# RWKV-7 inverse in 32x32 blocks, with the block transposes on VectorE

## The reference

```
S = S * w_t + (S a_t) b_t^T + v_t k_t^T        a_t = -kk_t, b_t = kk_t * iclr_t
y_t = S r_t                                    (latent tokens only)
w_t = exp(-exp(-softplus(-(w0 + tanh(wd) @ w2)) - 0.5)),  iclr_t = sigmoid(a0 + ad @ a2)
```

## Time and profile before

| | us |
|---|---|
| median of 3 runs | 1727.96 |
| lowest and highest | 1724.86, 1730.27 |
| span of the profiled execution | 1725.2 |
| TensorE busy (matmul) in that span | 1595.0 |
| VectorE, ScalarE, GpSimd busy | 706.5, 565.5, 871.3 |

### The profile page before, as it was taken

One profiled execution on the slowest core, in us unless ns is written; L12 is line 12 of the kernel. 1 busy time (PEld: TensorE's weight loads), 2 busy tenths in 40 slices (PEclk: granted clock), 3 DMA queues, 4 the chain that ended last, 5 costly groups with the idle time before them and its releaser, 6 DMA issues. The chain is left out here.

```text
span 1725.2 us, 35315 instructions
## 1 busy us (share of the span) xinstructions
PE 1595.0 (92%) x15534; PEld 1293.4 (75%) x15534; DVE 706.5 (41%) x1049; ACT 565.5 (33%) x810; POOL 871.3 (51%) x407
## 2 busy tenths in 40 slices
PE   4899999988989888989999999989989899999996
PEld 2688868767677786748888888858867588888885
DVE  1433246668676755462121212640374521212134
ACT  3423256543534322243232323132222432323230
POOL 1532213198776833248888888734433344444441
PEclk9999899999999999999999999889989999999998
DMA  7322001032222222224444443222221122222221
GB/s 319 125 77 78 1 1 50 2 116 86 101 77 77 79 75 81 74 74 147 146 147 146 146 146 146 73 74 98 92 78 50 64 102 94 93 93 96 96 94 49
DMA packets 23617, 162.15 MB, mean 94 GB/s; under 512 B 2624, under 2 KB 3264, under 8 KB 4800
## 3 DMA queue, kind: packets, MB, share of 16 engines
q1 hardware_dynamic: 21904, 154.09, 24.8%
q10 hardware_dynamic: 1584, 6.13, 0.9%
HBM read 157.71 MB, written 2.10 MB: 93 GB/s over the span
## 5 line engine op out<-in xcount | busy, mean ns | idle before, releaser
L221 POOL TENSOR_TENSOR v<-raw,v 128x1024 fp32r<-128x1024 f32 x160 | 389.7, 2459 | 421.6 <-ACT v L209 397.4
L238 PE MATMUL bank<-hm,v 128*128 128x512 f32 x2112 | 488.9, 393 | 15.0 <-DVE hm L1985 12.8
L238 PEld LDWEIGHTS bank<-hm,v 128*128 128x128 f32 x2112 | 400.0, 190 | 104.1 <-issue 17.8
L238 PE MATMUL bank<-hid,v 128*128 128x512 f32 x1536 | 349.5, 389 | 0.0
L238 PEld LDWEIGHTS bank<-hid,v 128*128 128x128 f32 x1536 | 288.3, 188 | 59.8
L209 ACT ACTIVATE v<-raw 128x2048 fp32r<-128x2048 f32 x77 | 147.6, 1917 | 420.8 <-PE bank L238 420.7
L2116 DVE TENSOR_TENSOR bank<-bank,rl 128x512 f32<-128x512 f32 x64 | 44.8, 700 | 275.1 <-ACT rl L2095 275.1
L1047 POOL TENSOR_TENSOR raw<-raw,cs 128x2048 f32<-128x2048 f32 x24 | 86.8, 3615 | 104.3 <-issue 64.3
L221 POOL TENSOR_TENSOR w<-raw,w 128x1024 fp32r<-128x1024 f32 x22 | 54.2, 2485 | 136.4 <-ACT w L209 136.4
L540 PE MATMUL bank<-h,w 128*128 128x512 f32 x600 | 109.6, 344 | 0.0
L540 PEld LDWEIGHTS bank<-h,w 128*128 128x128 f32 x600 | 93.9, 191 | 15.1 <-issue 1.1
(11 more groups left out here) (319 smaller groups left out, 2273.6 us busy)
## 6 DMA issues: line engine op xcount, KB each, us to landing
raw<-w_in SPq DMA_DIRECT2D x119, 1024.0 KB, 4.8
mraw<-wm_in SPq DMA_DIRECT2D x16, 1024.0 KB, 4.7
raw<-wm_in SPq DMA_DIRECT2D x3, 1024.0 KB, 16.2
xres<-x_in ACTq DMA_DIRECT2D x1, 2048.0 KB, 8.7
yb<-wm_in SPq DMA_DIRECT2D x2, 1024.0 KB, 19.6
mixed_in<-wm_in SPq DMA_DIRECT2D x2, 1024.0 KB, 23.5
xres<-x_in SPq DMA_DIRECT2D x1, 2048.0 KB, 8.9
out_T<-xres ACTq DMA_DIRECT2D x8, 256.0 KB, 2.0
```

The source lines that it names most:

```text
L221: i = nc.gpsimd.tensor_tensor(W[1][n % 2][:, k:k + 4], raw[n % 2][:, k:k + 4], W[0][n % 2][:, k:k + 4].bitcast(F32), SUB)
L238: last = nc.tensor.matmul(bank(b(s, m), 0, hi - lo), W[w][s][:, k, m * P:(m + 1) * P], H[h][:, k, lo:hi], start=(k == 0 and w == h == 0), ...
```

## The change

The inverse is taken in 32x32 blocks. Levels 0 to 3 (LVL = 4) invert only the diagonal 32x32 blocks: X, its transpose XTB and the level's product W1 have 384 elements a partition and direction instead of 768; products use 32 rows and 32 columns of TensorE each, 48 a group instead of 24, and all four row and column positions write one PSUM bank. The transpose of X is VectorE's 32x32 block transpose from SBUF to SBUF (`blocks_turned`); TensorE's transposes and ScalarE's `inverse_rows` go. The last level becomes two products: `corner_product` (the off-diagonal block of L times X) and `lower_columns` (the lower 32 columns of XT, with an identity that ScalarE puts beside the corner), each 24 products a direction; the left columns are a ScalarE copy with the upper half as scale.

In `chunk_matrices` item `L` computes diagonal 32x32 blocks alone (48 products instead of 24), and `LT` lies by head in the two banks. The low-rank products run two a level in levels 0 to 3, through banks 4, 5 and 7. ScalarE runs gates 0 to 4, the exponentials of direction 0, gates 5 and 6, the exponentials of direction 1, gate 7, the keys, then the left columns. The bonus product moves behind the corner products. The constant table is 191 columns narrower.

```diff
-    LVL = 5
+    LVL = 4
+    B = 32
...
+    def lora_at(i):
+        lo, hi = SEG[PIECES[i][1]]
+        return bank((4, 5, 7)[i % 3], 0, hi - lo)
...
-                if i:
-                    pe.wait_ge(sig_ready, NP * p + i)
-                nc.tensor.matmul(bank(7, 0, hi - lo), lw[r, p, kind, :], lora[r, kind, lo:hi], start=True, stop=True)\
-                    .then_inc(lora_done, 1)
+                if j:
+                    pe.wait_ge(sig_ready, NP * p + 2 * j - 1)
+                for d in range(2):
+                    r = slice(d * HD, (d + 1) * HD)
+                    nc.tensor.matmul(lora_at(2 * j + d), lw[r, p, kind, :], lora[r, kind, lo:hi], start=True, stop=True)\
+                        .then_inc(lora_done, 1)
...
+            def diagonal_blocks(i, d):
+                for g in range(GD):
+                    for c in range(2):
+                        for b in range(2):
+                            for h in range(2):
+                                at, cx = g * B, c ^ d
+                                t, ta = (2 * g + c) * Q + b * B, (2 * g + cx) * Q + b * B
+                                last = nc.tensor.matmul(ring(i, h, at, at + B)[quarter_of(cx, b)],
+                                                        AT_[half(h), d, ta:ta + B], BT[half(h), d, t:t + B],
+                                                        start=True, stop=True)
...
             def first_product(p, lv, d):
-                for g in range(GD):
+                for m in range(MS):
                     for q in range(2):
-                        for e in range(2):
-                            last = nc.tensor.matmul(bank(2 * d + e, g * Q, (g + 1) * Q)[half(q)], LT[half(e), d, g, q, :],
-                                                    X[half(e), d, g, q, :], start=True, stop=True)
+                        for b in range(2):
+                            r = quarter_of(q, b)
+                            last = nc.tensor.matmul(bank(2 * d, m * B, (m + 1) * B)[r], LT[r, d, m, b * B:(b + 1) * B],
+                                                    X[r, d, m, :], start=True, stop=True)
...
-            def transposes(p, lv, d):
...
+            def corner_product(p, d):
+                pe.wait_ge(x_ready, 2 * (LVL + 1) * p + 2 * LVL + d + 1)
+                for m in range(MS):
+                    for q in range(2):
+                        r = quarter_of(q, 0)
+                        last = nc.tensor.matmul(bank(2 * d, m * B, (m + 1) * B)[quarter_of(q, 1)], LT[r, d, m, B:Q],
+                                                X[r, d, m, :], start=True, stop=True)
+            def lower_columns(p, d):
...
+                        r = quarter_of(q, 1)
+                        last = nc.tensor.matmul(bank(2 * d + 1, m * B, (m + 1) * B)[half(q)], corner[r, d, m, :],
+                                                XTB[r, d, m, :], start=True, stop=True)
...
                 for lv in range(LVL):
                     first_product(p, lv, 0)
                     step(2 * lv + 1)
-                    transposes(p, lv, 0)
...
                     first_product(p, lv, 1)
-                    transposes(p, lv, 1)
+                    if p < PAIRS - 1:
+                        lora_pieces(p + 1, lv)
                     second_product(p, lv, 0)
                     step(2 * lv + 2)
                     second_product(p, lv, 1)
+                corner_product(p, 0)
+                step(2 * LVL + 1)
+                corner_product(p, 1)
+                bonus(p)
+                lower_columns(p, 0)
+                step(2 * LVL + 2)
+                lower_columns(p, 1)
...
+            def blocks_turned(p, lv, d):
+                dve.wait_ge(x_ready, 2 * (LVL + 1) * p + 2 * lv + d + 1)
+                nc.vector.transpose(XTB[:, d].rearrange("p m j -> p (m j)"), X[:, d].rearrange("p m j -> p (m j)"))\
+                    .then_inc(xt_ready, 1)
...
             def inverse(p):
+                corner_unit(p)
+                if p < PAIRS - 1:
+                    for i in range(NP):
                         gate(p + 1, i)
+                        if i == NP // 2:
+                            exponentials(p + 1, 0)
+                        if i == NP - 2:
+                            exponentials(p + 1, 1)
+                    keys(p + 1)
+                for d in range(2):
+                    left_columns(p, d)
```

More of the change, by code:

```diff
@@ L750, in build @@
     XM = sb(rw_sb, "XM", [P, 2, 2, GD, 2, Q])
-    XT, MT = XM[:, 0], XM[:, 1]
+    MT = XM[:, 1]
+    XT, corner = (XM[:, i].rearrange("p d g h j -> p d (g h j)").rearrange("p d (m j) -> p d m j", j=Q) for i in range(2))
     RKT = sb(rw_sb, "RKT", [P, 2, GL, 2, Q])
@@ L1108, in products @@
                             if kind == "LT":
[L1109 to L1111 removed]
+                                o, a, b = ring(i, h, at, at + Q)[half(cx)], BT[r, d, t], AT_[r, d, ta]
                             elif kind == "M":
@@ L1154, in chunk_matrices @@
                         last = masked_values(i, d)
+                    elif kind == "L":
+                        last = diagonal_blocks(i, d)
                     else:
@@ L1187, in second_product @@
             def second_product(p, lv, d):
-                n = 10 * p + 2 * lv + d
+                n = 2 * (LVL * p + lv) + d
+                pe.wait_ge(xt_ready, 2 * p + n + 1)
                 pe.wait_ge(w_ready, n + 1)
-                pe.wait_ge(xt_ready, 2 * n + 2)
-                for g in range(GD):
-                    for e in range(2):
-                        for q in range(2):
-                            xt, w = XT[half(q), d, g, e, :], W1[half(q), d, g, e, :]
-                            if lv < LVL - 1:
-                                last = nc.tensor.matmul(bank(2 * d + q, g * Q, (g + 1) * Q)[half(e)], xt, w, start=True,
-                                                        stop=True)
-                            else:
-                                last = nc.tensor.matmul(bank(2 * d + e, g * Q, (g + 1) * Q)[half(q)], w, xt, start=True,
-                                                        stop=True)
@@ L1202, in second_product @@
-                last.then_inc(s2_done, 1)
+                for m in range(MS):
+                    for q in range(2):
+                        for b in range(2):
+                            r = quarter_of(q, b)
+                            last = nc.tensor.matmul(bank(2 * d + 1, m * B, (m + 1) * B)[r], XTB[r, d, m, :],
+                                                    W1[r, d, m, :], start=True, stop=True)
+                last.then_inc(s2_done, 1)
+            def corner_product(p, d):
+                pe.wait_ge(x_ready, 2 * (LVL + 1) * p + 2 * LVL + d + 1)
+                for m in range(MS):
+                    for q in range(2):
+                        r = quarter_of(q, 0)
+                        last = nc.tensor.matmul(bank(2 * d, m * B, (m + 1) * B)[quarter_of(q, 1)], LT[r, d, m, B:Q],
+                                                X[r, d, m, :], start=True, stop=True)
+                last.then_inc(corner_done, 1)
@@ L1281, in results @@
                 pe.wait_ge(xf_ready, 2 * p + 2)
+                pe.wait_ge(left_ready, 2 * p + 2)
                 for k in range(3):
@@ L1567, in step @@
                         state_step(p - 1, s)
+                for d in range(2):
+                    blocks_turned(p, 0, d)
                 for lv in range(LVL):
```

151 lines of the change are left out of this document (69 added, 82 removed).

## The result

The changed kernel takes **1821.73 us** (median of 5 runs, 1805.67 to 1824.15) against 1730.27 us for the kernel before in the same series: a ratio of 1.052, 95% interval 1.048 to 1.056. The forecast was 1768 us with a range to 1802, so the direction was right and the size was not: +91 us where +40 was said. The execution that the profile shows took 1805.67 us, with a span of 1803.9; it is the fastest of the five.

What follows compares the result with a forecast made beforehand. TensorE's wait for 256-instruction blocks was taken as the bound: 42.8 for the inverse, -7.2 for blocks loaded ahead, +4 for chunk matrices, +39.6 on a span of 1725.2; with 2.8 us from span to median, 1768 us, range 1744 to 1802.

Steps and rivals of the forecast that it cites:

- blocks bound it: Inverse: TensorE waits for its program, which arrives in blocks of 256 instructions, one every 3.5 to 3.6 us; chance 0.82.
- the savings bought nothing: Levels: fewer transposes, ScalarE copies and halved VectorE work lie inside the wait for blocks, 8 us of chain against 11.
- 98 was said: RWKV part: instruction packets were to rise from 73 to about 98.
- the last pair grew most: Sign to look for: the four inverse stretches take about 47 to 53 us each, the last pair growing most.
- what was costed at nothing: VectorE's levels and the new order of ScalarE and GpSimd were taken as covered by the longer inverse: 0 us.
- The rival of 32x32 tiles that run one at a time: Levels: four tiles writing one PSUM bank take turns, a group lasting 2.8 us; +21 us, 1789 us; chance 0.05.
- 57.8 blocks x 3.6 us = 208.1 us: Four inverses: all their instruction blocks at one price, against 165.3 us before; +42.8 us.
- half a block a stretch: Inverse: each stretch begins with part of a block loaded ahead, taken as half a block; -7.2 us.
- The high end of 3.9 us: Inverse: slowest price of a block, 225.4 us or +60.1, with chunk matrices 10.8; 1799 us.
- chunk matrices +4: Chunk stages: 96 more records a pair, with room for them; 1.0 us a pair taken, between 0 and 2.7.
- 1764.8: Forecast span: 1725.2 us plus the summed terms, +39.6 us.
- the first rival: Blocks are not the bound, the chain decides and the inverses get shorter: -30.5 us together, 1697 us; chance 0.09.

Runs made afterwards that it cites:

- Run 2: Changed kernel with only every second product in the levels, each moving 64 columns, so half the instructions there and an inverse that is not real: 1734.97 us.
- run 3: Changed kernel with each 32x32 product of the levels moving 64 columns instead of 32, same number of instructions: 1816.13 us, ratio 1.049.
- run 4: Changed kernel with levels 1 and 2 using old operands, no wait for VectorE, and VectorE's work there left out: 1819.27 us.
- run 7: One last-pair group repeated: 33 times in the kernel before, 17 in the changed kernel, 17 in its 64-column version: 1774.89, 1870.34, 1868.40 us.
- run 5: Changed kernel with the earlier order of low-rank products and ScalarE (all gates, keys, then exponentials): 1826.76 us, ratio 1.057.
- run 10: Changed kernel with item L in 24 products of 64x64 tiles a direction instead of 48, lower blocks wrong: 1809.37 us.
- run 9: Changed kernel repeated, and with one 128x128x128 product ahead of each group of the levels to lift the clock: 1828.79 and 1824.43 us.
- run 8: Changed kernel with levels in 64x64 tiles on block-diagonal operands, 48 records a group: median 1797.02 us with 32 moving columns, 1734.93 us with 64.
- run 11: Item L left out, VectorE making the first X: 64x64 block-diagonal form 1755.92 us, kernel before 1765.07 us, the latter with its mask reading PSUM 1739.78 us.

## Why the prediction was right in its mechanism and wrong in its size

**Right: blocks bound it, and the savings bought nothing.** Packets rose to 99 (98 was said), "issue" heads TensorE's idle time, and the last pair grew most (36.7 to 61.8 us). Run 2 takes 24 blocks away and gets 86.8 us back, run 3 doubles the columns at no cost, run 4 drops VectorE's waits at no saving, and run 7 shows the stops after every 128 records with nothing else to wait for. The Trainium skill ("Runtime: NRT & Kernel Launch", Instruction fetch mechanics) has the cost of fetching mostly hidden; in this case dense small products show it in the open, a block every 3.48 us with TensorE busy for 11.67 of 20 us in run 7.

**Right: what was costed at nothing.** VectorE's level (run 4), ScalarE's and GpSimd's new order (run 5). The transpose lasts 0.573 us (0.5 was taken, 0.4 to 1.2 bounded). The rival of 32x32 tiles that run one at a time is out: 180 records in 1.78 us at full clock, 9.9 ns a record.

```profile
354.49 1.78 PE L1200 MATMUL bank<-xres 32*32 32x32 f32 x180 [0.90 <-ACT k_tok L1435]
```

**Wrong: "57.8 blocks x 3.6 us = 208.1 us".** One price was put on all blocks of the inverse; two kinds of stretch have other ones. (a) The tail, from the first corner product on. Its 7.9 blocks (57.8 less the 49.9 of the levels: 6384 records) were costed at 28.4 us, and take 51.1: +22.7. The prediction looked only at the number of instructions; it should have summed the work, state output, bonus, lower products on two tiles (1.59 to 2.77 us for 48 records), as for any stretch where few, long instructions stand. (b) The levels. 49.9 blocks less half a block a stretch were costed at 172.4 us and take 186.6 (from the first product to the first corner product: 48.2, 46.2, 45.2, 47.0): +14.2, or 3.88 us a block with the half block a stretch added back. Run 7 shows this as the pace of 32x32 products by themselves, 3.75 to 3.91 us; the 3.5 to 3.6 of the earlier trace rows had been read from 64x64 code, which run 7 puts at 3.48. The high end of 3.9 us covered (b), not (a) besides it.

**Wrong: "chunk matrices +4".** They took +8, 2 us a pair, inside the 0 to 2.7 that were given but twice what was taken. These stages had no room (run 10), and the identity's addition did not halve: L1555 has 1.82 us for 384 elements, against 2.39 us for 768. Inverse +36.9 over the sum, chunk stages +4: 1764.8 + 41 = 1806, and the span was 1803.9.

**Wrong: the execution and the median.** That kernel's times ran from 1806 to 1830 us over the two series, and the profiled execution was the fastest; 16 us of the miss against the median lie here. A second profile of the same program has a span of 1826.9 us, 23 more; 6.8 of them lie in the chunk stages and 4.9 in the inverses. It has longer chunk stages at a lower clock (pair 1: 26.7 us at 0.87, where the first has 23.4 at 1.00):

```profile
438.70:465.40 26.70, 19.25 (x657) 16.30 (x656) 13.29 (x14) 7.31 (x10) 25.92 (x14) 0.87 0.41 144
```

The prediction had no term for the clock at all. It shows in tails and, by this pair of profiles, perhaps in chunk stages; in the levels it costs little, by the two means of run 7 at most 0.16 us a block (3.91 less 3.75), 8 us in all. How much of the 16 us is the clock stays open, since run 9 did not move it far enough. A slip that changes nothing: the four gains of the first rival add up to 30.8 us, not 30.5.

## What to carry to other kernels

Count instructions before elements: here, where products were small, TensorE's program arrived in blocks of 256 instructions every 3.48 to 3.91 us, and halving the work of each product while doubling their number lost. Price each stretch by the larger of its blocks and its own busy time at the clock it will get, and take the pace of blocks from code of the same tile form. Moving the transposes from TensorE to VectorE bought nothing while TensorE's instruction count rose (changed kernel), no more than equalled the kernel before where the count fell a little (run 8). Giving VectorE the work of item L as well cost time, where all of its operands lay in SBUF beside a busy GpSimd (run 11).

## What the runs showed of the hardware that was not expected

- Dense 64x64 products got a block of 256 instructions every 3.48 us at clock 1.00, 32x32 ones every 3.75 us at clock 1.00 and 3.91 us at 0.50 (run 7).
- The granted clock was 0.55 to 0.64 in the changed inverse with 32x32 products of 32 columns, and 0.88 to 0.97 when the same instructions moved 64 columns (run 3). In the 64x64 form with 32 columns it went from 0.51 to 0.96 between one pair and the next, although TensorE was busy nearly all of the time in both; the two inverses differ by 26 us (run 8).
- Two of the four 64x64 tiles gave 48 records in 1.59 us at full clock, whether 32 or 64 columns moved (run 8); all four give 0.93 us. VectorE's transposes leave each block on its partitions, so both operands stay in the row half of the output, and the products are confined to the tiles of the diagonal (by the code; TensorE's transposes had been what spread them over four).
- VectorE's operations with both inputs in SBUF waited for GpSimd in run 11: 384 elements took 2.04 to 2.69 us against 0.555 us with one input in PSUM. In the last lines of run 11 VectorE's operations end at 351.78 and 354.40 us, each 0.42 us after the GpSimd operation beside it (351.36 and 353.98). The Trainium skill ("SBUF — State Buffer", SBUF: two separate sides) calls the pair of ports that these two share an exclusive lock, held for the whole instruction; this trace agrees.
